# Two fused transformer blocks in float32: the attention stages with joint norms, norm weights as columns, other stick-breaking passes, and new instruction orders

## What is computed

```python
for layer in range(2):
    h = rms_norm(x, mix_norm_g); proj = h @ w_in           # 2720 columns
    # diff_attention: 4 heads x 2 maps x 64; q and k each rms-normed over 64 (x weight)
    a = softmax(q0 k0 * 0.125 + bias) - lam * softmax(q1 k1 * 0.125 + bias);  o = a @ v
    o = rms_norm(o, subln_g) * (1 - lam_init)
    # stick_breaking: z = q k * 0.125, strictly causal
    later = reverse_cumsum(log_sigmoid(-z)) - log_sigmoid(-z);  a = exp(log_sigmoid(z) + later)
    # latent_attention
    q = rms_norm(c_q, cq_g) @ w_uq;  kv = rms_norm(c_kv, ckv_g) @ w_ukv    # ranks 256 and 128
    q, k = rms_norm(q, q_g), rms_norm(k, k_g)              # 4 heads x 96, last 32 of k shared
    q, k = rope(last 32 of each);  softmax(q k * 96 ** -0.5) @ v
    x = x + concat(y_a, y_b, y_c) @ w_out
    x = x + memory_attention(h, mem, ...)                   # keys and values from mem @ w_mem_kv
    x = x + square(relu(h @ w_ff1)) @ w_ff2
```

## Time and profile before

| | us |
|---|---|
| median of 3 timed runs | 3122.8 (3121.34 to 3122.99) |
| the profiled execution, whole | 3114.61 |
| its span, first to last instruction | 3112.8 |
| first attention stage, 2147.8 to 2299.7 | 151.9 |
| second attention stage, 2665.8 to 2818.0 | 152.2 |

### The profile page before, as it was taken

The page is one execution under the profiler, slowest core; times in us unless marked ns, Lnnn a source line. Parts: engine busy times, 40 slices in busy tenths (PEclk is TensorE's granted clock), DMA queues, the critical chain, the costliest instruction groups (busy, mean ns, idle before and its releaser), DMA issues.

```text
span 3112.8 us, 31727 instructions
## 1 busy us (share of the span) xinstructions
PE 2572.9 (83%) x11717; PEld 2004.8 (64%) x11717; DVE 2122.7 (68%) x2399; ACT 1553.6 (50%) x1899; POOL 41.5 (1%) x45
## 2 busy tenths in 40 slices
PE   5987599967947999999999999947676998666898
PEld 2736477856536777777777777836355886445687
DVE  6587586755655888887888878855764554675454
ACT  2223243432134878787787877834334443333443
POOL 0000000000100000000000000000000000000000
PEclk8997799986977999999999999978587998767799
DMA  8451256731333999898999989943022554103252
GB/s 256 130 189 42 81 191 240 275 119 59 101 104 131 333 339 334 309 359 296 342 332 343 331 294 351 354 141 125 0 78 76 172 188 140 63 10 112 82 189 95
DMA packets 275753, 599.63 MB, mean 193 GB/s; under 512 B 29371, under 2 KB 36339, under 8 KB 274437
## 3 DMA queue, kind: packets, MB, share of 16 engines
q1 hardware_dynamic: 252144, 580.30, 52.7%
q10 hardware_dynamic: 23446, 17.23, 2.0%
HBM read 596.39 MB, written 1.09 MB: 192 GB/s over the span
## 4 chain that ended last, share of the span: by engine, by line
PE 61%; DVE 24%; ACT 9%; issue 2%; ACTq 1%; DMA 1%; POOL 0%; DVEq 0%; POOLq 0%; PEldq 0%
PE PS L205 59%; DVE WL L167 6%; ACT WH L197 3%; DVE AR L167 2%; PE PS L213 2%; ACT AR L197 2%; DVE MOD L167 2%; DVE WF L167 1%; DVE MW L167 1%; ACTq L146 1%; ACT MW L197 1%; DVE SMALL L178 1%; DVE HF L167 1%; DVE HTR L167 1%; DVE AR L175 1%
## 5 line engine op out<-in xcount | busy, mean ns | idle before, releaser
L167 DVE TENSOR_TENSOR WL<-RG,WH 128x1024 fp32r<-128x1024 f32 (+1 forms) x558 | 919.4, 1648 | 494.3 <-ACT WH L197 471.1
L197 ACT ACTIVATE WH<-RG 128x1024 fp32r<-128x1024 f32 x782 | 827.3, 1058 | 630.3 <-PE PS L205 566.5
L205 PE MATMUL PS<-WH,HTR 128*128 128x512 f32 (+3 forms) x2920 | 929.4, 394 | 70.1 <-DVE HTR L167 24.5
L205 PEld LDWEIGHTS PS<-WH,HTR 128*128 128x128 f32 x2920 | 559.2, 194 | 206.1 <-DVE WL L167 37.2
L205 PE MATMUL PS<-WL,HTR 128*128 128x512 f32 (+3 forms) x1460 | 569.9, 390 | 0.0
L205 PE MATMUL PS<-WH,ATR 128*128 128x512 f32 x1624 | 523.1, 396 | 12.9 <-DVE ATR L167 7.3
L205 PEld LDWEIGHTS PS<-WH,ATR 128*128 128x128 f32 x1624 | 310.0, 191 | 80.9 <-DVE WL L167 14.6
L205 PE MATMUL PS<-MW,HTR 128*128 128x512 f32 x1332 | 329.7, 397 | 18.4 <-DVE MW L167 18.4
L205 PE MATMUL PS<-WL,ATR 128*128 128x512 f32 x812 | 320.4, 395 | 0.0
L205 PEld LDWEIGHTS PS<-WL,HTR 128*128 128x128 f32 x1460 | 283.7, 194 | 52.7
L167 DVE TENSOR_TENSOR MW<-RG,MW 128x2048 fp32r<-128x2048 f32 x112 | 256.7, 2292 | 65.1 <-ACT MW L197 54.5
(11 more groups left out here) (216 smaller groups left out, 2121.1 us busy)
## 6 DMA issues: line engine op xcount, KB each, us to landing
RG<-in_moe_w_gate SPq DMA_DIRECT2D x112, 1024.0 KB, 5.7
RG<-in_moe_w_up SPq DMA_DIRECT2D x112, 1024.0 KB, 5.9
RG<-in_moe_w_down SPq DMA_DIRECT2D x112, 1024.0 KB, 6.0
RG<-in_w_ff SPq DMA_DIRECT2D x64, 1024.0 KB, 5.2
RG<-in_mod_w SPq DMA_DIRECT2D x48, 1024.0 KB, 5.3
RG<-in_w_in SPq DMA_DIRECT2D x36, 1024.0 KB, 5.2
RG<-in_w_out SPq DMA_DIRECT2D x16, 1024.0 KB, 5.1
RG<-in_ffn_w_gate SPq DMA_DIRECT2D x14, 1024.0 KB, 5.5
```

The costliest lines, as they stand in the source:

```text
L167: return self.did(lambda: self.e.tensor_tensor(o, a, b, op))
L197: return self.did(lambda: self.e.activation(o, a, f, bias=bias, scale=scale))
L205: return self.did(lambda: self.e.matmul(o, l, r, start=start, stop=stop))
```

## The change

It touches five places.

1. `v_rsqrt` takes four instructions for five, everywhere.
2. Differential attention: the squares of q and k go to ACT, q and k are normed in one pass over 1024 columns per tile, the norm weights (q's times k's times 0.125 as far as they act on q) become a column `G_DA` that is applied when the transposed q is copied from PSUM. The softmax factors no longer scale the exponentials: the second map is scaled by lam times the ratio of the sums in one instruction per head, and the reciprocal of the first sum is applied at the output copy.
3. Latent attention: c_q and c_kv are transposed without being normed; their weights are columns used when the transposes are copied, and their factors are applied to the products. The copies of kv go to ACT. The squares of q and k go to ACT, and norm, weight and rope run once over both (1536 columns) in place of twice.
4. Stick-breaking: five passes over z become two. Memory keys: all scaling copies from PSUM (twelve of 256 columns) go from DVE to ACT.
5. `a_rows2` issues eight DMAs for twelve, `a_second_in` thirteen for seven. All strings of `ORDERS` are new except those of POOL; no piece is added in `start`, `mixers0`, `mixers1`.

```diff
 ORDERS = {
-    ("attention0", "a"): "dbckdkdcddbbdcdbdbddbbcccbbdckbdcdcdbcdbbccckc",
-    ("attention0", "pe"): "ddcbkbdbdcdcccdccbbbddddddbbbbddbcdbcdccddccdddddbdcbbckccbbccckkbbkbckkckcccccccckk",
-    ("attention0", "v"): "dddcbbbdbddcdccdcbcddbccddbcdbcdbcdkkcccbddckddddddcbcddbckkcckkbkdbcbcckckckc",
+    ("attention0", "a"): "ddbkcckdkcbbcdcdbcbddccbbddcbbdccbdbcbdcdckkdkkbckk",
+    ("attention0", "pe"): "ddcccbkcbcbccdddbbbdccbbddccbbddbddbddbdccccdccccccbbbbbddcbccdddddcdccckbkbkcckkkkkk",
+    ("attention0", "v"): "kddbcddcbbkccbcdckdbdcbdcdcbcddccbdbdcdcbcdbcccdbddddcdbcddcbdbcckkk",
...
+    ("attention1", "a"): "dckbcdkdbcbkccddbcdbdccbbddcbbcdcbdbcbdcdckkdkkbckk",
...
         def v_rsqrt(v, dst, st, n):
             v.rcp(dst, t)
-            v.tt(t, dst, dst, MUL)
-            v.tt(t, t, m, MUL)
-            v.ts(t, t, -0.5, 1.5, MUL, ADD)
-            return v.tt(dst, dst, t, MUL)
+            v.tt(t, dst, m, MUL)
+            v.stt(t, t, -0.5, dst, MUL, MUL)
+            return v.stt(dst, t, 1.5, dst, ADD, MUL)
...
         def a_second_in(a):
+            for i, n in enumerate(("da_q_norm_g", "da_k_norm_g")):
+                for h in range(2):
+                    a.dma(CB[64 + 2 * i:66 + 2 * i, 256 + 64 * h:320 + 64 * h], w[n + "_2"]).then_inc(gc_in)
+            a.dma(CB[68:72, 256:384], ...).then_inc(gc_in)     # mla_cq_norm_g
+            a.dma(CB[72:74, 256:384], ...).then_inc(gc_in)     # mla_ckv_norm_g
             a.dma(RW, w["moe_w_router"][0].rearrange("(k p) e -> p k e", p=128)).then_inc(rt_in)
...
         def v_diff(v, l):
-            v.ts(ROWS[:, R_DQ:R_DQ + 64], ROWS[:, R_DQ:R_DQ + 64], 0.125, None, MUL)
-            v_rms_begin(v, da_v, "rq", DAQ, 8, 64, view(DSC[:, :, 0:512], 8), DST, D_AT)
+            yield
+            v.wait_ge(da_a, l, "sq")
+            v.red(r.rearrange("p (t n) -> p t n", t=2), view(DSQ, 16), ADD)
+            v_root(v, D_AT, r, 1.0 / 64, 1e-6, 32).then_inc(da_v, "rqk")
...
-            v_rms_end(v, da_a, l, "rq", DAQ, 8, 64, gains(R_DQ, 8, 64), DST, D_AT).then_inc(da_v, "q")
-            v_rms_begin(v, da_v, "rk", DAK, 8, 64, view(DSC[:, :, 0:512], 8), DST, D_AT)
-            yield
-            v_rms_end(v, da_a, l, "rk", DAK, 8, 64, gains(R_DK, 8, 64), DST, D_AT).then_inc(da_v, "k")
+            v.wait_ge(da_a, l, "rqk")
+            v_rsqrt(v, r, D_AT, 32)
+            v.tt(DQK, DQK, r...broadcast_to([128, 2, 16, 64]), MUL).then_inc(da_v, "qk")
...
-            v.cp(DQT[:, 0:2, :], pair(0)).then_inc(da_v, "tq0")
+            v.ts(DQT[:, 0:2, :], pair(0), G_DA[:, l:l + 1], None, MUL).then_inc(da_v, "tq0")
...
                 for h in range(4):
-                    v.ts(su[:, 4 + h:5 + h], su[:, 4 + h:5 + h], LAM[:, 0:1], None, MUL)
...
-                    v.ts(AM[:, h, 0:wdt], ET[:, h, 0:wdt], su[:, h:h + 1], None, MUL, None)
-                    v.stt(AM[:, h, 0:wdt], ET[:, 4 + h, 0:wdt], su[:, 4 + h:5 + h], AM[:, h, 0:wdt], MUL, ADD).then_inc(
+                    v.stt(AM[:, h, 0:wdt], ET[:, 4 + h, 0:wdt], s2[:, h:h + 1], ET[:, h, 0:wdt], MUL, ADD).then_inc(
                         da_v, f"am{t}{h}")
...
-                v.cp(H[:, t, 0:512], PS[:, 2, :]).then_inc(da_v, f"o{t}")
+                v.tt(DAO[:, t], PS[:, 2, :]..., r1.unsqueeze(2).broadcast_to([128, 4, 128]), MUL).then_inc(da_v, f"o{t}")
...
         def a_diff(a, l):
+            for t in range(2):
+                x = a.act(DSQ[:, t], PR2[:, t, 0:1024], ACT.Square)
+            x.then_inc(da_a, "sq")
...
                     if t:
                         a.wait_ge(da_v, l, "am03")
+                        a.wait_ge(da_v, l, "o0")
...
         def v_keys(v, l):                      # the same twelve copies now in a_keys, as ACT.Copy with a column scale
-                    x = v.ts(METR[:, 2 * i + k, :], PS[:, i % 2, k * 256:(k + 1) * 256], gcol(3, l)[...], None, MUL)
...
-                v.ts(KM[:, t, :], PS[:, t, 0:256], sm(MST + t, 1), None, MUL)
...
-                v.ts(VM[:, t, :], PS[:, t, 256:512], sm(MST + t, 1), None, MUL)
...
         def v_stick(v, l):
-                v.ts(cs, zz, 0.0, None, MAX, None)
-                v.ts(zz, zz, 0.0, None, MIN)
-                v.tt(zz, zz, lg, SUB)
-                v.tt(lg, cs, lg, ADD)
-                v.ts(lg, lg, -1.0, None, MUL)
+                v.stt(cs, zz, 0.0, lg, MIN, SUB)
+                v.stt(lg, zz, 0.0, lg, MAX, ADD)
...
         def pe_latent(pe, l):
-            pe.wait_ge(la_v, l, "cq")
             pe_transposes(pe, PR2[:, :, 2304:2560], 2, (5,), lambda k0: (la_pe, "cq"))
...
         def v_latent(v, l):
+            v.cp(LK[:, :, :, 64:96], PR2[:, :, 2688:2720].unsqueeze(2).broadcast_to([128, 2, 4, 32]))
+            v.tt(CSC, PR2[:, :, 2304:2688], PR2[:, :, 2304:2688], MUL)
+            ...                                 # two reductions, two eps, one v_rsqrt of four
...
-            rope(LQ).then_inc(la_v, "q")        # twelve instructions of 64 columns
-            v_rms_begin(v, la_v, "rk", LK, 4, 96, view(LSC[:, :, 0:384], 4), LST, L_AT)
-            yield
-            v_rms_end(v, la_a, l, "rk", LK, 4, 96, gains(R_MK, 4, 96), LST, L_AT)
-            rope(LK).then_inc(la_v, "k")        # twelve more
+            v.tt(k16, k16, r.unsqueeze(2).broadcast_to([128, 16, 96]), MUL)      # 1536 columns
+            v.tt(k2, k2, ROWS[:, R_MQ:R_MQ + 192]..., MUL)                       # 1536 columns
+            ...                                 # rope: six instructions of 256 columns
-            v.ts(LQT[0:96], LQT[0:96], 96.0 ** -0.5, None, MUL).then_inc(la_v, "scaled")
...
         def a_latent(a, l):
+                a.act(LK[:, t, :, 0:64], p4[:, :, 0:64], ACT.Copy, scale=sm(LST + 2 + t, 1))
+                a.act(VV[:, t, :]..., p4[:, :, 64:128], ACT.Copy, scale=sm(LST + 2 + t, 1))
+            a.act(LSC, AR[:, 12608:14144], ACT.Square).then_inc(la_a, "sq")
```

More of the change, by code:

```diff
@@ L2245, in build @@
         DSC = two(AR[:, 11584:12608])
-        DAQ, DAK = (view(PR2[:, :, z * 512:(z + 1) * 512], 8) for z in range(2))
+        DQK, DSQ = view(PR2[:, :, 0:1024], 16), two(AR[:, 5440:7488])
         DAO = view(H[:, :, 0:512], 4)
@@ L2444, in v_keys @@
             v.wait_ge(mm_a, l, "nrt")
[L2445 to L2452 removed]
+            v_rsqrt(v, sm(MST, 2), M_AT, 2).then_inc(mm_v, "rs")
             yield
[L2454 to L2456 removed]
+            v.wait_ge(mm_a, l, "k")
             v.wait_ge(rows_in, ROWS_OF[2 + l])
@@ L2459, in v_keys @@
             v.stt(ROWS[:, R_EK:R_EK + 64], ROWS[:, R_EK:R_EK + 64], 0.125, ROWS[:, R_EQ:R_EQ + 64], MUL, MUL)
-            for t in range(2):
-                v.ts(VM[:, t, :], PS[:, t, 256:512], sm(MST + t, 1), None, MUL)
             yield
@@ L2477, in a_keys @@
             a_root(a, M_AT, 2).then_inc(mm_a, "nrt")
+            for i in range(4):
+                yield
+                a.wait_ge(mm_pe, l, f"np{i}")
+                for k in range(2):
+                    x = a.act(METR[:, 2 * i + k, :], PS[:, i % 2, k * 256:(k + 1) * 256], ACT.Copy,
+                              scale=gcol(3, l)[:, 2 * i + k:2 * i + k + 1])
+                x.then_inc(mm_a, f"ng{i}")
+            yield
+            a.wait_ge(mm_v, l, "rs")
+            a.wait_ge(*W.of["mem_kv", l][-1].raw)
+            for t in range(2):
+                x = a.act(KM[:, t, :], PS[:, t, 0:256], ACT.Copy, scale=sm(MST + t, 1))
+            x.then_inc(mm_a, "k")
+            for t in range(2):
+                a.act(VM[:, t, :], PS[:, t, 256:512], ACT.Copy, scale=sm(MST + t, 1))
             yield
@@ L2651, in pe_latent @@
                 pe.wait_ge(la_a, l, k)
-            pe.wait_ge(la_v, l, "scaled")
+            for k in ("tq0", "tk0"):
+                pe.wait_ge(la_v, l, k)
             qf, kf, wdt_of, v_of = latent_maps()
@@ new lines, in v_latent @@
+            v.wait_ge(la_a, l, "sq")
+            r = sm(LST + 4, 16)
+            v.red(r, LSC.rearrange("p (n d) -> p n d", d=96), ADD)
+            v_root(v, L_AT, r, 1.0 / 96, 1e-6, 16).then_inc(la_v, "rqk")
+            v.wait_ge(rows_in, ROWS_OF[2 + l])
+            yield
+            v.wait_ge(la_a, l, "rqk")
+            v_rsqrt(v, r, L_AT, 16)
+            k16 = KQZ.rearrange("p z (h d) -> p (z h) d", h=4)
+            v.tt(k16, k16, r.unsqueeze(2).broadcast_to([128, 16, 96]), MUL)
+            k2 = KQZ.rearrange("p (a t) (h d) -> p a (t h) d", a=2, h=4)
@@ new lines, in v_latent @@
+            v.tt(k2, k2, ROWS[:, R_MQ:R_MQ + 192].rearrange("p (a d) -> p a d", a=2).unsqueeze(2).broadcast_to([128, 2, 8, 96]), MUL)
+            x1, x2 = KQ6[:, :, :, 64:80], KQ6[:, :, :, 80:96]
+            tab = KC[:, K_ROPE:K_ROPE + 128].rearrange("p (z n) -> p z n", z=4)
+            co, si = (tab[:, :, c:c + 16].unsqueeze(2).broadcast_to([128, 4, 4, 16]) for c in (0, 16))
+            s4 = [LSC[:, i * 256:(i + 1) * 256].rearrange("p (z h n) -> p z h n", z=4, h=4) for i in range(4)]
+            v.tt(s4[0], x1, co, MUL)
```

178 lines of the change are left out of this document (83 added, 95 removed).

## The result

The changed kernel takes 3038.3 us (median of four runs, 3035.6 to 3042.0) where the kernel before takes 3122.8 (3121.3 to 3123.0 beside it): a ratio of 0.9731, with an interval of 0.9714 to 0.9748. That is 84.5 us less; the forecast was 64.7 less (3058, range 3026 to 3092).

What follows compares the result with a forecast made beforehand. DVE was taken to bound the two attention stages. Attention -61.4, `a_rows2` -3.9, `a_second_in` +2.8 and `v_rsqrt` elsewhere -1.6 sum to -64.1 us, from 3122.8 to 3058.7, say 3058; own range 3040 to 3076, wider range 3026 to 3092.

Steps and rivals of the forecast that it cites:

- The bound: Attention stages: DVE bounds them; 32.4 us of its busy time go per layer, leaving DVE and PE even.
- The chain: Each attention stage as five consecutive intervals of dependent work: 121.2 us against 151.9, so 30.7 saved per layer.
- I4: Attention stage, memory keys and values, from tile 1's differential output to the end of their last product: 26.2 to 22.5 us.
- I5: Attention stage tail, from the end of the memory keys' and values' last product to stage end: 12.6 to 9.3 us.
- I3: Attention stage, from tile 1's first differential scores to the end of its output: 48.0 to 35 us.
- I2: Attention stage, from tile 0's first differential scores to tile 1's first: 38.4 to 27.0 us.
- I1: Attention stage, from its start to tile 0's first differential scores: no gain, 26.8 to 27.4 us.
- `a_rows2`: ACT's DMA issues ahead of the norm stages' first copy: four fewer save 1.9 us, twice 3.9.
- `a_second_in`: ACT's DMA issues at the second block's gating stage: six more at 0.48 us each cost 2.8 us.
- 1: Attention stages: longer joint pieces in the queues eat the gain, each stage gaining only 13 to 17 us; 3088 us, chance 0.21.
- 2: Attention stages: denser work raises PE's clock to full, score groups halve, 14 us more per layer; 3030 us, chance 0.16.
- 3: Attention stages: slower, as a late memory tensor shifts the stage one us per us late; 3135 us, chance 0.04.

Runs made afterwards that it cites:

- keys_dve: The changed kernel with the twelve scaled copies of the memory's keys and values back on DVE: 3055.4 us, ratio 0.9794 to the kernel before.
- rows_12: The changed kernel with four unread norm-row DMAs back in ACT's queue ahead of each attention layer, twelve issues for eight: 3040.9 us, ratio 0.9752 to the kernel before.
- warm_scores: The changed kernel with extra unread matmuls on PE in its waits around the differential score groups: 3028.5 us, ratio 0.9709 to the kernel before.

## Why the prediction was right, and where its sizes were off

**The bound.** Right in its sizes: 32.4 us of DVE's busy time went from each stage (82 forecast to stay, 81.3 measured). That this shortened the stages is shown for a part. Undoing three pieces, stick-breaking's passes, the softmax factors and the keys' copies (13.0 of the 32.4 us), gave back 17.6 us in the first stage and 17.7 in the second, of the 35.9 and 40.0 that were won. The norms of the differential and latent strands (18.5 us) were not undone, nor was the new order tried by itself, so how much of the rest belongs to less work and how much to the order is open. ACT came to 56.3 (56 forecast), table loads to ten and eleven (ten and twelve). A scalar-tensor pass costs what the two-tensor price says (1.226 us for 1024 columns), and the joint passes of 2048 and 1536 columns 2.291 and 1.757 (2.29 and 1.76 forecast).

**The chain.** Its form held in all five intervals; 121.2 was forecast and 116.0 and 112.2 came. Of the 14.2 us that were missing, these terms are the ones mis-sized:
- I4, 5.7 us in both layers. The first product began 5.7 us after o1 (5.5 forecast). The step that failed is "17 us of products as before". The 17 held pieces of other strands and a first group of eight products that took 5.37 us behind a wait of PE, at the lower clock for the most part. In the new order they ran in 13.97 at the higher level throughout. keys_dve shows both halves: with a wait of 4.3 us ahead they took 16.06.
- I5, 3.7 us. The terms for transposes (1.7) and handovers (1.5) were too large; the four transposes took 1.1 and the gaps between the steps came to 0.75 in the first stage.
- I3, 2.2 us. s10 was priced at the lower level (9.2) and took 4.8. Only a part of that came through: from s10's end to s11 it took 5.4 where 4.6 was forecast, and from s11's end to o1's end 14.8 for 13.2; the 35 that was taken was also 1.2 under its own steps, which sum to 36.2.
- I2, 2.1 us, from errors both ways. s01 was priced at 4.6 and took 5.9, and its exponentials ended 18.9 us after s00 began (17.4 forecast). From there to s10 it took 7.3 where 9.6 was forecast.
- I1, 0.5 us. +1.1 in the first layer, where stick-breaking's pass began 22.3 us after the start (21.3 by the forecast's steps) behind a wait for ACT's logarithm, and -1.6 in the second, where the copy of the k transposes stands ahead of the stick-breaking pass. That the root stands behind the memory's squares was seen; that the landing varies by 2 us from run to run was not, though in the second layer of the kernel before the tensor landed 7.9 us after its issue and not 5.6.

**Outside.** `a_rows2`: 3.9 forecast, 3.9 measured in the two norm stages with `v_rsqrt` in them, and rows_12 gives 3.8 for the issues alone. `a_second_in`: 2.8 forecast; PE's wait grew from 10.44 to 12.34, 1.9. The step that failed is the price of an issue, 0.48 each. ACT's timeline there:

```profile
868.82 0.61 ACTq L146 DMA_DIRECT2D CB<-in_da_q_norm_g  x2
869.46 0.57 ACTq L146 DMA_DIRECT2D CB<-in_da_k_norm_g  x2
870.06 0.28 ACTq L146 DMA_DIRECT2D CB<-in_mla_cq_norm_g  x1
```

The six small ones cost 0.31 each with the gap behind them, not 0.48. The strings of the first block: 0 forecast, nothing shown (`start` ended at 133.7 us before, and at 131.0 to 134.1 in the kernels with the new strings). The 5.9 us by which the profiled execution was longer there are scatter, and with them the 79.0 of the spans come near the 84.5 of the medians.

**The rivals.** 1 did not come: no stage over 117. 2 came in part. The stage's clock rose to 0.75 and 0.79, under the 0.8 that was to mark it, with one of the four score groups and the keys at the higher level. The four groups of the changed kernel sum to 26.0 us against 27.8 before, so the rise of s10 was half eaten by the fall of s01; the prediction, which halves all four for this rival, missed that s01 already stood at the higher level before. The rest was to be had: warm_scores took the first stage to 109.4 at 0.89. The Trainium skill, TensorE: Matmul & The Clock Gate, HAM oscillation, tells of waits between groups of matmuls that throw the clock back each time. The trace agrees: s01 and s11, behind waits, ran at the lower level, and s10, which had no wait ahead of it, at the higher. The inference that I2 and I3 would therefore stay low as a whole did not hold, as the new order left s10 without its wait. 3 came as a mechanism in small: 2 us of landing, 2.3 us of the second stage. The tensor was not alone on its queue, as the prediction has it (two weights, 640 KB together, are issued beside it), but so it is in every run here, late or not. `v_rsqrt` was not tried by itself.

That the measured time lies 20 us under the forecast, and yet inside the range, owes something to luck: errors both ways offset each other within I2 and I3, and a part of the gain of I4 came from a clock that the forecast had left as it was.

## What to carry to other kernels

When an engine that feeds PE gets faster, count twice: the waits that vanish, and the clock of the PE work behind them (s10 took 5.0 us for 9.3 once PE no longer stood idle ahead of it). It works both ways: products moved out of a wait of PE left s01 at the lower level, 5.9 us for 3.4. A duration of a group taken over from the old trace is good only if its wait ahead and its neighbours stay. And in a stage written out as strings, the length of one profiled stage says little until its landing times and its clock are compared with those of the other run.
